# Whole f32 projections replaced by three split products, with high and low parts made in the kernel

## What is computed

```python
hs = adaln(xs, norm1_g[l], ss1, cs1)            # rmsnorm(x) * g * (1 + scale) + shift
q, k, v = jnp.split(h @ w, 3, axis=-1)          # 8 heads, q and k of 2 x 64, v of 128
qs, ks_ = apply_axial_rope(qs, cos, sin), apply_axial_rope(ks_, cos, sin)
s = jnp.einsum('bqhcd,bkhcd->bhcqk', qi, k)     # latent queries see latent and cached keys
p = jax.nn.softmax(s, axis=-1)
a = p[:, :, 0] - lam * p[:, :, 1]
o = jnp.einsum('bhqk,bkhe->bqhe', a, v)
o = rmsnorm(o, g) * (1.0 - lam_init)
mixed = o.reshape(b, n, ATTN_WIDTH) @ wo
m = jax.nn.silu(cvec) @ w + b                   # modulation: shift, scale, gate of all sub-layers
```

## Time and profile before

| | |
|---|---|
| time, median of 3 runs | 3680.73 us (3679.54 to 3680.92) |
| profiled execution | 3688.61 us, span 3686.8 us |
| PE busy | 3348.8 us, 91% of the span |
| DVE busy | 1480.3 us, 40% |
| ACT busy | 807.6 us, 22% |
| POOL busy | 629.1 us, 17% |
| line 554, projection of q, k, v | 391.4 us on PE, 1152 records |
| line 958, output projection | 127.2 us on PE, 288 records |
| line 538, modulation adds on POOL | 321.1 us, 112 of 2.89 us |

### The profile page before, as it was taken

The page is one execution under the profiler, slowest core; times in us unless marked ns, Lnnn a source line. Parts: engine busy times, 40 slices in busy tenths (PEclk is TensorE's granted clock), DMA queues, the critical chain, the costliest instruction groups (busy, mean ns, idle before and its releaser), DMA issues. The chain is left out here.

```text
span 3686.8 us, 57439 instructions
## 1 busy us (share of the span) xinstructions
PE 3348.8 (91%) x23344; PEld 2949.3 (80%) x23344; DVE 1480.3 (40%) x2471; ACT 807.6 (22%) x1794; POOL 629.1 (17%) x526
## 2 busy tenths in 40 slices
PE   7999999997893999999999997274999999999995
PEld 3666666765453999999999997164999999999995
DVE  2455555553356333333333332865333333333332
ACT  2555555565110001001011011220010010110111
POOL 1333333443110000001001001530000010010011
PEclk9999999997895999999999999586999999999997
DMA  5222222122235877877877872156778778778783
GB/s 194 76 77 77 77 75 73 59 67 95 89 113 197 281 261 253 293 257 262 289 251 272 288 242 96 50 197 228 258 253 292 257 263 290 249 272 290 240 276 115
DMA packets 408715, 722.85 MB, mean 196 GB/s; under 512 B 15985, under 2 KB 319762, under 8 KB 408626
## 3 DMA queue, kind: packets, MB, share of 16 engines
q1 hardware_dynamic: 397010, 682.75, 53.5%
q0 software_dynamic: 11616, 38.94, 4.1%
HBM read 673.40 MB, written 48.23 MB: 196 GB/s over the span
## 5 line engine op out<-in xcount | busy, mean ns | idle before, releaser
L1328 PE MATMUL bank<-ex_xT,ring 128*128 128x144 f32 x11264 | 1391.1, 287 | 5.6 <-DVE ex_xT L1404 5.6
L1328 PEld LDWEIGHTS bank<-ex_xT,ring 128*128 128x128 f32 x11264 | 1387.5, 191 | 6.4 <-issue 5.8
L1345 PE MATMUL bank<-ex_hid,ring 128*128 128x144 f32 x5632 | 698.5, 287 | 0.0
L1345 PEld LDWEIGHTS bank<-ex_hid,ring 128*128 128x128 f32 x5632 | 691.6, 190 | 0.9
L538 POOL TENSOR_TENSOR acc<-acc,prod 128x1280 f32<-128x1280 f32 x112 | 321.1, 2889 | 560.7 <-ACT prod L731 560.7
L554 PE MATMUL bank<-wh,hT 128*128 128x384 f32 x1152 | 391.4, 494 | 0.0
L1368 ACT ACTIVATE ex_ge<-bank 128x432 f32<-128x432 f32 (+1 forms) x128 | 64.0, 500 | 1307.7 <-PE bank L1328 1307.7
L1284 POOL DMA_INDIRECT xres_lat<-ex_ye,ex_si x32 | 51.9, 1623 | 1748.3 <-ACT ex_ye L1382 1748.3
L554 PEld LDWEIGHTS bank<-wh,hT 128*128 128x128 f32 x1152 | 214.2, 191 | 165.8 <-issue 32.0
L1418 DVE RECIPROCAL ex_t<-ex_t 128x432 f32<-128x432 f32 (+1 forms) x128 | 336.4, 2628 | 4.5
L1417 DVE TENSOR_SCALAR ex_t<-ex_ge 128x432 f32<-128x432 f32 (+1 forms) x128 | 46.9, 366 | 664.4 <-ACT ex_ge L1368 664.4
(11 more groups left out here) (197 smaller groups left out, 2443.6 us busy)
## 6 DMA issues: line engine op xcount, KB each, us to landing
ring<-in_expert_w_gate SPq DMA_DIRECT2D x96, 1536.0 KB, 8.7
ring<-in_expert_w_up SPq DMA_DIRECT2D x96, 1536.0 KB, 12.3
ring<-in_expert_w_down SPq DMA_DIRECT2D x96, 1536.0 KB, 12.4
ring<-in_expert_w_gate SPq DMA_DIRECT2D x32, 1024.0 KB, 6.1
ring<-in_expert_w_up SPq DMA_DIRECT2D x32, 1024.0 KB, 8.6
ring<-in_expert_w_down SPq DMA_DIRECT2D x32, 1024.0 KB, 18.3
wmr<-in_w_mod SPq DMA_DIRECT2D x64, 384.0 KB, 3.7
wmr<-in_w_mod SPq DMA_DIRECT2D x64, 256.0 KB, 3.1
```

Of the source, the lines that this page charges most:

```text
L1328: last = nc.tensor.matmul(bank[:, banks[j % 2], f * CAP:(f + 1) * CAP], wv[:, c, f * P:(f + 1) * P], xT[:, c], start=(c == 0), stop=(c == ...
L1345: last = nc.tensor.matmul(bank[:, YB[m // 3], (m % 3) * CAP:(m % 3 + 1) * CAP], wv[:, q, m * P:(m + 1) * P], hid[:, f], start=(f == 0), st ...
```

## The change

Every operand of the two projections is split into a high part, rounded to the type F32R, and a low part, the rest. A product then becomes three F32R products into the same sum: high by high, high by low, low by high.

- hT becomes hTh and hTl. DVE writes the modulated f32 piece to a scratch tile (hfull, four pieces), ACT copies it to hTh, DVE (even pieces) or POOL (odd pieces) subtracts to get hTl. The lambda sums move between the first and the second eight pieces.
- wh becomes wraw, whh and whl; whl takes the place of wraw. ACT rounds (four copies of 768 columns per head) and DVE subtracts: for head 0 at the stage's start, for head 1 in the projections 2 to 5 of head 0, for head h + 2 in the steps 2 to 5 of head h. PE waits for the low parts.
- wo becomes woh (POOL, in the last head, after its adds) and wol (DVE); its load is issued in step 64.
- oT becomes oTh (ACT) and oTl (DVE, behind the residual update of the tile before).
- To make room, qT has one buffer instead of two, the rotation tables hold 64 columns instead of 128 and are read twice, and an output tile is stored by a DMA per step from one of two buffers. SP's list is written by steps instead of by heads.

```diff
-        hT, wh_at = sb("hT", [P, DC, N_TOK], persistent_end)
-        wh, wh_end = sb("wh", [P, 2, DC, 3 * VD], wh_at)
+        hTh, wh_at = sb("hTh", [P, DC, N_TOK], persistent_end, F32R)
+        hTl, wh_at = sb("hTl", [P, DC, N_TOK], wh_at, F32R)
+        whl, wh_end = sb("whl", [P, 2, DC, 3 * VD], wh_at, F32R)
+        wraw, _ = sb("wraw", [P, 2, DC, 3 * VD], wh_at)
+        whh, wh_end = sb("whh", [P, 2, DC, 3 * VD], wh_end, F32R)
...
+                def low_part(eng, ops, n):
+                    t0, nt = ((0, 4), (4, 4), (8, 1))[n // DC]
+                    c = n % DC
+                    eng.wait_ge(hi_ok, n + 1)
+                    cols = slice(t0 * P, (t0 + nt) * P)
+                    ops.tensor_tensor(hTl[:, c, cols], hfull[:, n % 4, 0:nt * P], hTh[:, c, cols].bitcast(F32),
+                                      ALU.subtract).then_inc(lo_ok[n % 2], 1)
...
+                    def high_part(n):
+                        t0, nt = ((0, 4), (4, 4), (8, 1))[n // DC]
+                        act.wait_ge(hT_ok, n + 1)
+                        nc.scalar.activation(hTh[:, n % DC, t0 * P:(t0 + nt) * P], hfull[:, n % 4, 0:nt * P], ACT.Copy
+                                             ).then_inc(hi_ok, 1)
...
+                        for c in range(DC):
+                            dve.wait_ge(xT_mm, n + 1)
+                            if n >= 4:
+                                dve.wait_ge(lo_ok[n % 2], (n - 4) // 2 + 1)
+                            nc.vector.tensor_scalar(hfull[:, n % 4, 0:nt * P], bank[:, n % 8, 0:nt * P],
+                                                    gains[:, 0, c, cond:cond + 1],
+                                                    modc[:, SHIFT1 * DC + c, cond:cond + 1], ALU.mult, ALU.add
+                                                    ).then_inc(hT_ok, 1)
+                            n += 1
+                            if n >= 2 and n % 2 == 0:
+                                low_part(dve, nc.vector, n - 2)
...
+                    for k in range(STEPS + 1):
+                        h, n = k // TT, k % TT
+                        if k < STEPS and n + 1 < DC:
+                            load_wm(h, n + 1)
...
+                        if k == STEPS - LT:
+                            sp.wait_ge(S["qkv_mm"], STEPS)
+                            sp.dma_start(wo[:], a["attn_wo"][0].rearrange("(h p) d -> p h d", p=P)).then_inc(wo_in, 16)
+                        if k:
+                            store_o(k - 1)
...
+                            if h == H - 1 and c >= 2:
+                                high_wo(c - 2)
...
-                            last = nc.tensor.matmul(bank[:, qkv_bank(g), 0:3 * VD], hT[:, c, t * P:(t + 1) * P], wh[:, h % 2, c],
-                                                    start=(c == 0), stop=(c == DC - 1))
+                            if t == 0 and c % 2 == 0:
+                                pe.wait_ge(w_lo[h % 2], 4 * (h // 2) + c // 2 + 1)
+                            for i, (x, w) in enumerate(((hTh, whh), (hTh, whl), (hTl, whh))):
+                                last = nc.tensor.matmul(bank[:, qkv_bank(g), 0:3 * VD], x[:, c, t * P:(t + 1) * P], w[:, h % 2, c],
+                                                        start=(c == 0 and i == 0), stop=(c == DC - 1 and i == 2))
...
+                    def high(h, i):
+                        act.wait_ge(w_in[h % 2], 48 * (h // 2 + 1))
+                        if h >= 2:
+                            act.wait_ge(S["qkv_mm"], TT * (h - 1))
+                        nc.scalar.activation(whh[:, h % 2, 2 * i:2 * i + 2], wraw[:, h % 2, 2 * i:2 * i + 2], ACT.Copy
+                                             ).then_inc(w_hi[h % 2], 1)
...
                         if k + TT < STEPS:
                             values(k + TT)
+                        if 2 <= n < 6 and k < STEPS and h + 2 < H:
+                            high(h + 2, n - 2)
                         if k < STEPS and n < DC:
                             products(h, n)
...
+                    def low(h, i):
+                        dve.wait_ge(w_hi[h % 2], 4 * (h // 2) + i + 1)
+                        nc.vector.tensor_tensor(whl[:, h % 2, 2 * i:2 * i + 2], wraw[:, h % 2, 2 * i:2 * i + 2],
+                                                whh[:, h % 2, 2 * i:2 * i + 2].bitcast(F32), ALU.subtract).then_inc(w_lo[h % 2], 1)
...
                             rotate(k + TT)
+                        if 2 <= n < 6 and h + 2 < H:
+                            low(h + 2, n - 2)
+                        if h == H - 1 and n >= 4:
+                            low_wo(n - 4)
...
+                            for c in range(H):
+                                for i, (x, w) in enumerate(((oTh, woh), (oTh, wol), (oTl, woh))):
+                                    for b in range(2):
+                                        last = nc.tensor.matmul(bank[:, b0 + b, :], x[:, t % 2, c], w[:, c, b * 512:(b + 1) * 512],
+                                                                start=(c == 0 and i == 0), stop=(c == H - 1 and i == 2))
...
+                    def oT_low(t):
+                        dve.wait_ge(S["oT_hi"], t + 1)
+                        if t >= 2:
+                            dve.wait_ge(S["mm_done"], t - 1)
+                        nc.vector.scalar_tensor_tensor(oTl[:, t % 2].rearrange("p (b c) n -> p b (c n)", b=2), bank[:, 2:4, :], sub8[:],
+                                                       oTh[:, t % 2].rearrange("p (b c) n -> p b (c n)", b=2).bitcast(F32),
+                                                       ALU.mult, ALU.subtract).then_inc(S["oT_ok"], 1)
...
                             nc.vector.memset(st1[:, s, 4:5], 0.0).then_inc(S["tmp_ok"], 1)
+                        if attn and s + 1 < TT:
+                            oT_low(s + 1)
```

More of the change, by code:

```diff
@@ L8 @@
 F32 = mybir.dt.float32
+F32R = mybir.dt.float32r
 U32 = mybir.dt.uint32
@@ L309, in _ @@
                         root(t)
+                    for n in range(1, 3 * DC, 2):
+                        low_part(pool, nc.gpsimd, n)
                 @block.vector
@@ new lines, in _ @@
+                    dve.wait_ge(mod_ok, NT + 2)
+                    n = 0
+                    for g, (t0, nt) in enumerate(((0, 4), (4, 4), (8, 1))):
+                        if g == 1:
+                            dve.wait_ge(s_lam, 64)
+                            dve.wait_ge(ssq_ok, TT)
+                            step.link(nc.vector.tensor_tensor_reduce(sq[:, 0:HD], lrow[:, 0], lrow[:, 1], 1.0, 0.0, ALU.mult,
+                                                                     ALU.add, lsum[:, 0:1]))
+                            nc.vector.tensor_tensor_reduce(sq[:, 0:HD], lrow[:, 2], lrow[:, 3], 1.0, 0.0, ALU.mult, ALU.add,
+                                                           lsum[:, 1:2]).then_inc(ssq_ok, 1)
+                        cond = 1 if t0 == LT else 0
+                        for c in range(DC):
[9 more added lines that the diff above has]
+                                low_part(dve, nc.vector, n - 2)
@@ L451, in attention @@
                 o_out = [sem(st, f"at_o_out{i}") for i in range(2)]
+                w_hi = [sem(st, f"at_w_hi{i}") for i in range(2)]
+                w_lo = [sem(st, f"at_w_lo{i}") for i in range(2)]
                 block = st.enter_context(nc.Block())
@@ L731, in products @@
                             nc.scalar.activation(dst, wm[:, i % 2], ACT.Copy, scale=silu[:, cond, c:c + 1]).then_inc(S["prod_ok"], 1)
+                    def high(h, i):
[4 more added lines that the diff above has]
+                                             ).then_inc(w_hi[h % 2], 1)
+                    for i in range(4):
+                        high(0, i)
                     cache_out(0)
@@ L735, in _ @@
                         values(g)
+                        if 2 <= g < 6:
+                            high(1, g - 2)
                         if g:
@@ L825, in _, with low_wo @@
                         rotate(g)
+                        if 2 <= g < 6:
+                            low(1, g - 2)
+                    def low_wo(i):
+                        dve.wait_ge(wo_hi, i + 1)
+                        nc.vector.tensor_tensor(wol[:, i], wo[:, i], woh[:, i].bitcast(F32), ALU.subtract).then_inc(wo_lo, 1)
                     for k in range(STEPS):
```

146 lines of the change are left out of this document (64 added, 82 removed).

## The result

The changed kernel takes 3690.99 us (median of ten runs, 3685.45 to 3698.16), the kernel before 3680.82 in the same runs: a ratio of 1.0025, 95% interval [1.0016, 1.0035]. It is slower by 10.2 us where I had forecast faster by 12.6.

A forecast was written before the change was run, and what follows sets the result against it. PE was taken to bound first projection and mixer, PE and the ring tied the heads. 16.4 - 1.7 - 11.9 + 8.7 - 1.0 - 23.1 = -12.6 us from the median 3680.7 gave 3668 us, range 3648 to 3688.

The forecast's parts named there:

- gain 3.43 each: Mixer: each of nine output tiles takes 10.3 us instead of 13.7, a gain of 3.43, together -30.9 us.
- wait for the last add and move with it: Heads' ends: the sums wait for POOL's last add and shift with it; no change in their length was counted.
- the F32R product: Both projections: one product takes a quarter of an f32 pair, 165 ns for 384 columns and 214 for 512.
- the ring: Heads: the chain of line 807, rotation, V, ACT's products and POOL's add needs 10.88 us, 11.70 with ACT's copy.
- the two bounds: Heads: PE and the ring are tied at a step of 11.02 us; a faster PE buys 0.13 us a step.
- the first projection: Stretch up to 114.7 us: nine tiles gain 1.32 us each, all on PE, together -11.9 us.
- The head of the program: Setup: splitting hT costs +16.4 us (bounds +14 and +18.5), the halved tables give -1.7, together +14.7.
- The heads: Heads: +8.7 us; six with ACT's copy +10.2, the seventh without it -1.5, the last 0.
- The mixer: Mixer: -23.1 us, from -30.9 in nine output tiles and +7.8 in waits for DVE's low half.
- rival 1: Setup and heads: setup and ACT's copies cost somewhat more, giving 3676 us, no difference; chance 0.24.
- rival 2: Heads: the ring doesn't hold, PE's saving counts in 63 later tiles, -83 instead of +8.7, 3576 us; chance 0.06.
- rival 3: Both projections: an F32R product takes as long as one whole record, +273 us in all, 3954 us; chance 0.08.

The follow-up runs named there:

- adds_dve: The changed kernel with the additions of the modulation products moved from POOL to DVE: 3602.15 us, ratio 0.9782 to the kernel before.
- before_copies: The kernel before with only ACT's copies added, 768 columns into an unread spare tile in steps 2 to 5 of six heads: 3700.91 us, ratio 1.0055.
- second executions: The changed kernel and the kernel before, both unchanged, run once more to read their stages: 3691.65 and 3680.72 us.
- before_adds_dve: The kernel before with the additions of the modulation products moved from POOL to DVE: 3675.52 us, ratio 0.9984.
- high_first: The changed kernel with each output tile's 32 products on the high half first, so it starts without the low half: 3675.74 us, ratio 0.9981.
- narrow: high_first with output products of 256 columns instead of 512, 96 a tile instead of 48: 3680.28 us in one run.

## Why the prediction was wrong

The sum missed by 23.5 us, +10.9 for -12.6, and two of its steps failed. It held times fixed that move with TensorE's granted clock: the output tiles, which "gain 3.43 each", and the sums at a head's end, which "wait for the last add and move with it". The runs show 9.3 us more lost to half clock in the tiles and sums that are 9.5 us longer. And it mis-sized the F32R product: 173 and 233 ns where it had 165 and 214, 10.5 us together. Setup, ring and the rest came out some 6 us better than forecast.

**What bounds the kernel.** Right in what follows from it: PE's saving did not come through in the heads, and the ring did it (`adds_dve`). By the rule of the Trainium skill that I cited, page "SBUF — State Buffer", section "Who interferes with whom", the tiny DVE operation stands for a whole POOL instruction; the 2.96 us of line 858 agree. Wrong in a detail: the two bounds were not tied in the sense that the ring held PE. PE issued a projection 3.3 us after the V that it waits for, and the ring could be lengthened for four steps before PE noticed (`before_copies`). For the same reason the sign that I gave, PE waiting in each of the steps 2 to 5, did not come: it waits from a head's fifth projection on.

**The F32R product.** One pass, as taken, but 173 and 233 ns instead of 165 and 214. That costs 9 x 24 x 8 ns = 1.8 us of the first projection, most of its miss of 2.8, and 8.7 us of the mixer: an output tile at full clock takes 11.43 us, not 10.47 (13.90 - 3.43), so nine tiles gain 22.2 and not 30.9. The other 1.0 us of the first projection is a reading of mine: the 330 ns between f32 records is the mean of a tile whose second record starts 427 ns after the first, while all others start 322 to 323 apart. A quarter of a pair was 161 ns and the tile 0.11 us shorter than I took it, nine times.

**The head of the program.** +12.8 for +14.7. DVE's last operation ends at 70.78, 15.2 us later than before for the 16.4 of the sum. The timeline of DVE in the changed kernel's setup:

```profile
49.18 0.69 DVE L243 TENSOR_TENSOR hTl<-hfull,hTh 128x512 fp32r<-128x512 f32 x1 [2.57 <-ACT hTh L285]
49.79 1.52 DVE L384 TENSOR_SCALAR hfull<-bank,gains,modc 128x512 f32<-128x512 f32 x2
51.29 0.69 DVE L243 TENSOR_TENSOR hTl<-hfull,hTh 128x512 fp32r<-128x512 f32 x1
...
56.12 0.22 DVE L375 CUSTOM_DVE_ANT_0 sq<-lrow 128x64 f32<-128x64 f32 x1
...
56.38 1.24 DVE L377 CUSTOM_DVE_ANT_0 sq<-lrow 128x64 f32<-128x64 f32 x1
...
66.77 0.78 DVE L243 TENSOR_TENSOR hTl<-hfull,hTh 128x128 fp32r<-128x128 f32 x1
...
70.62 0.16 DVE L393 TENSOR_SCALAR nlam<-lsum 128x1 f32<-128x1 f32 x1
```

It stood for ACT's first copy until 49.18 (forecast 49.05); a pair takes 2.11 and not 2.29 us, since two writes take 1.52 us where I had 1.64; and POOL's subtractions got in the way twice, on line 377, 1.24 us where its twin of line 375 took 0.22, and on the first narrow subtraction, 0.78 us where the next ones took 0.29.

**The heads.** +15.6 for +8.7. The ring was right and its place in PE's steps half wrong. From a head's first add to its last it is 68.2 us instead of 66.1, +2.1 where I had +2.5. Counted by the starts of line 858, a head of 105.56 us is 2.76 over one of 102.81, of which the first three steps give -2.6 (I had -0.75 in the first two, +0.68 in the third), the next four +1.65, the last but one, where line 858 stands 2.9 us under the add instead of 0.7, +2.1, and the last, which holds the sums, +1.7. With sums at full clock the head is 102.3 long, less than before. The step that failed is the one that says that the sums move with the last add: it left their length as it was, and they are 9.5 us longer in the seven heads, which is more than the miss of 6.9.

That the wait ahead of the sums brings this is argued; no run changes the wait alone. In the second executions the sums took 5.6 to 6.9 us behind waits of about 0.15 us (kernel before) and 7.0 to 8.1 behind 1.2 to 2.7 (changed kernel), and 5.4 to 8.2 behind 1.7 in the heads with copies of `before_copies`. But a wait is not needed for half clock: in `before_adds_dve` PE doesn't wait there, and the seven heads' sums still took 5.0 to 5.1 us at granted clocks of 0.86 to 0.89.

**The mixer.** -6.0 for -23.1: 8.7 us are the longer product, the gaps are +6.8 for +7.8 (of which 1.3 belong ahead of the first tile, outside this stretch; the terms add up to 7.7), and 9.3 us are half-clock stretches in tiles (the nine tiles' excess over 11.43 is 11.8 us; over 13.90 it was 2.4 before). The sentence on the mixer gave the granted clock as a property of the stage, near full; the change itself took it away in most tiles. `high_first` shows it: with the gaps of before, seven of nine tiles keep full clock. The shorter products have a part in it, as its tile 2 shows.

**The sum and the median.** That the median lies 7.9 us under the profiled execution did not carry over. Part of the 7.9 stood in stages that the change doesn't touch, and the changed kernel has a scatter of its own, from the heads' ends. The rivals missed as well: rival 1 has the right sign of its costs, but not their size; rival 2 came true only once the adds were off POOL (heads of 743.0 us, 76 under before, for the 83 that it named); rival 3 fell with the first records of the product. None of them had the clock, and the rival on the slower side should have been that one: 0.6 us or more of gap ahead of each tile and sums that wait for an add at each head's end were in my own sum.

## What to carry to other kernels

Where a product is made faster and something else keeps its pace, TensorE waits. Here the new waits came with more time at half clock on top, in the sums (52.6 us for 43.1) and in the output tiles (11.8 us over full clock for 2.4). Look for the places where PE will newly stand, and order its work so that it can start on what is there (the high half here). If two chains are about equally long, shorten the one that isn't being worked on first: the same move of the adds was worth 6 us before the change and 89 after it. A forecast of a few tenths of a per cent needs the stages of more than one execution.

## What the hardware showed that I had not expected

- An F32R product moves 0.451 to 0.456 ns a column at a granted clock of 1.00, over 256 to 512 columns, where f32 records, with two cycles a column at 2.4 GHz, start 322 ns apart for 384 columns and 429 for 512: 0.42 ns a column and pass. At half clock the 384 columns stood 320 ns apart, 0.833 a column, exactly one a cycle of 1.2 GHz. Why F32R falls 8 to 9% short of a column a cycle at 2.4 GHz stays open; a fixed time for each product explains at most 3.5 ns of it (`narrow`).
- The same sequence of 40 sums took 4.6 us or up to 8.5, by the granted clock alone, and the same nine output tiles with the same gaps 141 to 150 us of mixer. With PE's waits in the heads gone (`adds_dve`) five runs lay within 1.8 us, where ten of the changed kernel spread over 12.7.
- A copy of 0.83 us added to a chain that a step waits for left the step unchanged at 11.02 us, and came out at the head's end, 30 to 65 us later.
